# The attention layer of a two-layer decoder trunk: head pairs written out, score tiles in groups of two, and fp32 products on 64x64 blocks

## The reference

```python
kvf = rmsnorm(h, kv_norm) @ kv_w
k_sh = head_rmsnorm(kvf[..., :D].reshape(B, T, N_HEADS, HEAD_DIM), k_norm)
v_sh = kvf[..., D:2 * D].reshape(B, T, N_HEADS, HEAD_DIM)
c_all = jnp.cumsum(jax.nn.log_sigmoid(kvf[..., 2 * D:] + kv_f_bias), axis=1)
...
proj = rmsnorm(h, norm) @ w_in
q = head_rmsnorm(proj[..., :D].reshape(B, S, N_HEADS, HEAD_DIM), q_norm)
z = proj[..., D:]
logits = q @ k.T * scale + cq[..., None] - ck[:, :, None, :]
p = softmax(where(key_pos <= q_pos, logits, -inf))
out = h + ((p @ v) * silu(z)) @ w_out
```

## Time and profile before

| | us |
|---|---|
| median of 3 runs | 2184.94 (2183.36 to 2185.37) |
| the profiled execution's own time | 2185.29 |
| its span, first to last instruction | 2183.6 |
| TensorE busy | 1980.7 |
| VectorE busy | 1026.8 |
| ScalarE busy | 1011.5 |
| GpSimd busy | 239.0 |

### The profile page before, as it was taken

One profiled execution on the slowest core, in us unless ns is written; L12 is line 12 of the kernel. 1 busy time (PEld: TensorE's weight loads), 2 busy tenths in 40 slices (PEclk: granted clock), 3 DMA queues, 4 the chain that ended last, 5 costly groups with the idle time before them and its releaser, 6 DMA issues.

```text
span 2183.6 us, 58287 instructions
## 1 busy us (share of the span) xinstructions
PE 1980.7 (91%) x24895; PEld 1699.7 (78%) x24895; DVE 1026.8 (47%) x1967; ACT 1011.5 (46%) x1735; POOL 239.0 (11%) x253
## 2 busy tenths in 40 slices
PE   5699999999999999999699699999999999998798
PEld 4688988888898988888498477777777777777477
DVE  3656566666666565665523633333333333333421
ACT  3445444444445454444311436464646555565511
POOL 0011111111111111111000201011010101010000
PEclk9899999999999999999689889999999999999799
DMA  5101010000101010100142101010000101000233
GB/s 196 49 2 44 8 36 18 24 27 17 36 8 44 8 46 8 37 15 22 64 139 70 61 21 29 30 29 29 19 29 19 39 10 39 19 29 10 77 116 116
DMA packets 103578, 89.46 MB, mean 41 GB/s; under 512 B 3973, under 2 KB 95736, under 8 KB 103112
## 3 DMA queue, kind: packets, MB, share of 16 engines
q1 hardware_dynamic: 100120, 68.50, 10.7%
q0 software_dynamic: 3040, 17.14, 2.0%
q10 hardware_dynamic: 208, 0.66, 0.1%
HBM read 64.96 MB, written 21.33 MB: 40 GB/s over the span
## 4 chain that ended last, share of the span: by engine, by line
PE 75%; DVE 9%; ACT 8%; issue 5%; DMA 2%; ACTq 0%; SPq 0%; DVEq 0%; POOLq 0%
PE ps L1666 6%; PE ps L1978 6%; PE ps L1979 6%; PE ps L1980 6%; PE ps L2055 5%; PE ps L1668 5%; PE ps L1667 5%; PE ps L1770 4%; PE ps L1602 3%; PE ps L1604 2%; PE ps L1603 2%; PE ps L1799 2%; PE ps L2013 2%; PE ps L2039 2%; PE ps L1794 2%
## 5 line engine op out<-in xcount | busy, mean ns | idle before, releaser
L1666 PE MATMUL ps<-xh,wh 128*128 128x258 f32 (+1 forms) x1024 | 327.8, 320 | 7.5 <-ACT arena L871 3.5
L1667 PE MATMUL ps<-xh,wl 128*128 128x258 f32 (+1 forms) x1024 | 291.0, 284 | 0.0
L1668 PE MATMUL ps<-xl,wh 128*128 128x258 f32 (+1 forms) x1024 | 290.8, 284 | 0.0
L1978 PE MATMUL ps<-xh,wh 128*128 128x348 f32 x768 | 260.1, 339 | 19.8 <-ACT arena_b L1096 14.5
L1979 PE MATMUL ps<-xh,wl 128*128 128x348 f32 x768 | 254.6, 332 | 0.0
L1980 PE MATMUL ps<-xl,wh 128*128 128x348 f32 x768 | 253.9, 331 | 0.0
L1551 DVE TENSOR_REDUCE arena_b<-ps 128x1 f32<-128x144 f32 (+4 forms) x224 | 106.7, 505 | 269.4 <-PE ps L2017 156.8
L1666 PEld LDWEIGHTS ps<-xh,wh 128*128 128x128 f32 x1024 | 193.3, 189 | 26.0 <-ACT arena L871 5.9
L1667 PEld LDWEIGHTS ps<-xh,wl 128*128 128x128 f32 x1024 | 194.1, 190 | 2.6
L2055 PE MATMUL ps<-arena_b 128*128 128x512 f32 (+4 forms) x448 | 186.3, 500 | 9.8 <-ACT arena_b L1120 9.8
L1668 PEld LDWEIGHTS ps<-xl,wh 128*128 128x128 f32 x1024 | 193.5, 189 | 0.0
(11 more groups left out here) (252 smaller groups left out, 4359.7 us busy)
## 6 DMA issues: line engine op xcount, KB each, us to landing
wr<-in_w_in SPq DMA_DIRECT2D x33, 512.0 KB, 4.1
xt_scr<-arena POOLq DMA_DIRECT2D x2, 4176.0 KB, 13.3
wr<-in_kv_w SPq DMA_DIRECT2D x16, 512.0 KB, 4.0
wr<-in_b_w_in SPq DMA_DIRECT2D x16, 512.0 KB, 3.8
arena<-xt_scr SPq DMA_DIRECT2D x8, 522.0 KB, 4.6
arena<-oa_scr SPq DMA_DIRECT2D x8, 520.0 KB, 3.6
arena<-in_x SPq DMA_DIRECT2D x8, 512.0 KB, 3.5
wr<-in_w_out SPq DMA_DIRECT2D x8, 512.0 KB, 3.7
```

The source lines that it names most:

```text
L1666: pe.matmul(bank, wh[:, j, k, :], xh[:, k, t], start=(k == 0), stop=False)
L1667: pe.matmul(bank, wl[:, j, k, :], xh[:, k, t], start=False, stop=False)
L1668: mm = pe.matmul(bank, wh[:, j, k, :], xl[:, k, t], start=False, stop=(k == KO - 1))
L1978: pe.matmul(bank[:, 0:SEG], wh[:, slot, k, :], xh[:, k, t], start=(k == 0), stop=False)
```

## The change

It does the following, in the attention layer alone:

- The loop over pairs is written out on all engines.
- The 14 units of a head go in eight groups (`GROUPS`), mostly of two. The order is: what `fill` holds for the group, the scores of the next group into both score banks, then the weighted sums of this group. The scores of a group wait for all exponentials of the one before. `pt` has four buffers.
- A projection chunk is issued in two halves of 12 products, between which other steps can stand.
- A weighted sum over 128 keys becomes four products of 64 keys by 64 output rows, on the four 64x64 blocks of the array. The two halves of the keys go to two banks, `B_PV[0]` and `B_PV[1]`, and both banks serve every query block. At the end of a block ScalarE copies the first bank to `ob` and `den`, and VectorE adds the second.
- Ln and Exp of the sum of weights are done once per head over 1024 columns, beside those of the sums of squares (`den`, `rsq`). The gate is applied head by head (`gated`), and each head's half is stored by itself.
- A sum of squares is two products on the two diagonal 64x64 blocks.
- `stack` is cut into `stackk` and `stackq`, and all steps get new places.

```diff
-        ARENA_B = 12780
+        ARENA_B = 13848
...
-        pt = [carve_b(512) for _ in range(3)]
-        dln = carve_b(512)
-        ob = carve_b(SEQ)
+        pt = [carve_b(512) for _ in range(4)]
+        ob, den = carve_b(SEQ), carve_b(SEQ)
...
+        GROUPS = [(0, 1), (2, 3), (4,), (5, 6), (7, 8), (9, 10), (11, 12), (13,)]
+        def proj(j, i, *between):
+            return [("proj", j, i, 0), *between, ("proj", j, i, 1)]
         def order(e, more):
...
+            maxima = iter([("smax", 1 - e, i) for i in range(NS)])
+            def m(n):
+                return [next(maxima) for _ in range(n)]
+            fill = [[] for _ in GROUPS]
+            if e == 0:
+                fill[0] = [("vrow", 1, 0), ("vrow", 1, 1), ("stackk", 1), ("stackq", 1)]
+                if more:
+                    fill[1] = proj(0, 0)
+                    fill[2] = m(2) + proj(0, 1, *m(2))
+                    fill[3] = m(2) + proj(0, 2, *m(2))
+                    fill[4] = ([("sumsq", 0, i) for i in range(3)] + [("den", 1), ("rsq", 0)] + m(1) + proj(1, 0, *m(2)))
+                    fill[5] = [("norm", 0)] + m(2) + proj(1, 1, *m(1))
+                    fill[6] = [("maxrow", 1)] + proj(1, 2) + [("gated", 1)]
+                    fill[7] = [("gate",)]
+                else:
+                    fill[1] = [("wsplit",)]
+                    fill[2] = m(3)
+                    fill[3] = m(3) + [("orow", 0)]
+                    fill[4] = m(3) + [("den", 1), ("orow", 1)]
+                    fill[5] = m(3) + [("gated", 1), ("orow", 2)]
+                    fill[6] = m(2) + [("gate",), ("orow", 3)]
+                    fill[7] = [("maxrow", 1)]
+            elif more:
+                fill[0] = [("sumsq", 1, i) for i in range(3)] + [("den", 0), ("rsq", 1)] + proj(2, 0) + [("stackk", 0)]
+                fill[1] = proj(2, 1) + [("norm", 1), ("stackq", 0)]
+                fill[2] = proj(2, 2) + [("gated", 0)]
+                fill[3] = [("vrow", 0, 0), ("vrow", 0, 1)] + m(2) + proj(3, 0, *m(2))
+                fill[4] = m(2) + proj(3, 1, *m(2))
+                fill[5] = m(2) + [("proj", 3, 2, 0)] + m(2)
+                fill[6] = m(2) + [("wsplit",)]
+                fill[7] = [("maxrow", 0), ("proj", 3, 2, 1)]
+            else:
                 for i in range(3):
...
+                    fill[1 + i] = [("orow", 4 + i)]
+                fill[2] = [("den", 0), ("gated", 0)] + fill[2]
+            steps = [("scores", e, 0)]
+            for g in range(len(GROUPS)):
+                steps += fill[g]
+                if g + 1 < len(GROUPS):
+                    steps += [("scores", e, g + 1)]
+                steps += [("weighted", e, g)]
             return steps
...
-            def store_ob(p, dst):
-                pool.wait_ge(S.o_gated, p + 2)
-                pool.dma_start(dst, ob).then_inc(S.ob_stored, 16)
-                pool.wait_ge(S.ob_stored, 16 * p + 16)
+            def store_ob(p, e):
+                pool.wait_ge(S.o_gated, 2 * p + e + 2)
+                pool.dma_start(ob_scr[p][head(e), :], ob[head(e), :]).then_inc(S.ob_stored, 16)
+                pool.wait_ge(S.ob_stored, 16 * (2 * p + e) + 16)
                 pool.sem_inc(S.ob_free, 1)
             for j in range(2, 4):
                 scale_b(0, j)
             scale_b(1, 0)
...
+            for p in range(KO - 1):
+                scale_b(p + 1, 1)
+                scale_b(p + 1, 2)
+                if p:
+                    store_ob(p - 1, 1)
+                scale_b(p + 1, 3)
+                store_ob(p, 0)
+                if p + 2 < KO:
+                    scale_b(p + 2, 0)
...
-                        if i == 2:
-                            act.wait_ge(S.b_evac, n_ + 1)
-                            act.activation(brs, brs, ACT.Exp, scale=-0.5).then_inc(S.hn_rstd, 1)
-                    elif kind == "stack":
+                    elif kind == "den":
+                        n_ = 2 * (p - st_[1]) + st_[1]
+                        if n_ >= 0:
+                            act.wait_ge(S.pv_free, 4 * n_ + 4)
+                            act.activation(den[head(st_[1]), :], den[head(st_[1]), :], ACT.Ln).then_inc(S.d_ln, 1)
+                            if ("rsq", 1 - st_[1]) not in steps:
+                                act.wait_ge(S.d_ln, n_ + 1)
+                                act.activation(den[head(st_[1]), :], den[head(st_[1]), :], ACT.Exp, scale=-1.0)\
+                                    .then_inc(S.d_recip, 1)
+                    elif kind == "rsq":
+                        j = st_[1]
+                        act.wait_ge(S.b_evac, chunk(p, (L_SK, L_SQ)[j]) + 3)
+                        act.activation(brs, brs, ACT.Exp, scale=-0.5).then_inc(S.hn_rstd, 1)
+                        n_ = 2 * p - 1 + j
+                        if ("den", 1 - j) in steps and n_ >= 0:
+                            act.wait_ge(S.d_ln, n_ + 1)
+                            act.activation(den[head(1 - j), :], den[head(1 - j), :], ACT.Exp, scale=-1.0)\
+                                .then_inc(S.d_recip, 1)
+                    elif kind == "stackk":
...
+                        if p + e > 0:
+                            act.wait_ge(S.pv_done, NU * (2 * p + 1 - e))
...
+                        e, g = st_[1:]
+                        for i, w in enumerate(GROUPS[g]):
+                            n_k, q0, n_q, _, _ = unit(w)
+                            n_ = NU * (2 * p + e) + w
+                            act.wait_ge(S.st_done, n_ + 1)
+                            if n_ >= 4:
+                                act.wait_ge(S.pv_done, n_ - 3)
+                            act.activation(pt[n_ % 4][0:n_k, 0:n_q], ps[0:n_k, B_ST[i], 0:n_q], ACT.Exp,
+                                           scale=SCALE).then_inc(S.p_exp, 1)
                     elif kind == "weighted":
-                        e, w = st_[1:]
+                        e, g = st_[1:]
+                        w = GROUPS[g][-1]
                         qb_, kt = UNITS[w]
                         if kt == 4 * qb_ + 4:
                             b, o = slice(e * HD, (e + 1) * HD), slice((1 - e) * HD, (2 - e) * HD)
-                            n_ = 4 * p + 2 * e + qb_
-                            act.wait_ge(S.pv_done, 2 * NU * p + NU * e + w + 1)
-                            act.wait_ge(S.o_norm, n_ + 2)
-                            act.activation(dln[b, :], ps[o, B_PV[qb_], :], ACT.Ln).then_inc(S.d_ln, 1)
-                            act.wait_ge(S.d_ln, n_ + 1)
-                            act.activation(dln[b, :], dln[b, :], ACT.Exp, scale=-1.0).then_inc(S.d_recip, 1)
-
-            def c_rows_of(head):
-                return c_scr[bass.ds(head, 1)].rearrange("a b t -> (a b) t")
+                            c = slice(qb_ * 512, (qb_ + 1) * 512)
+                            if qb_ == 0:
+                                act.wait_ge(S.ob_free, max(2 * p + e, 1))
+                                if p:
+                                    act.wait_ge(S.o_scaled, 2 * p + e - 1)
+                            act.wait_ge(S.pv_done, NU * (2 * p + e) + w + 1)
+                            for dst, rows_ in ((den[b, c], o), (ob[b, c], b)):
+                                act.activation(dst, ps[rows_, B_PV[0], :], ACT.Copy).then_inc(S.pv_read, 1)
...
-                            b = slice(e * HD, (e + 1) * HD)
-                            dve.wait_ge(S.d_recip, 4 * p + 2 * e + qb_ + 1)
-                            if e == 0 and qb_ == 0:
-                                dve.wait_ge(S.ob_free, p + 1)
-                            dve.tensor_tensor(ob[b, qb_ * 512:(qb_ + 1) * 512], ps[b, B_PV[qb_], :], dln[b, :], ALU.mult)\
-                                .then_inc(S.o_norm, 1)
-                            if e and qb_:
-                                dve.wait_ge(S.o_norm, 4 * p + 6)
-                                dve.wait_ge(S.bz_gate, p + 1)
-                                dve.scalar_tensor_tensor(ob, ob, 0.5, zg[:, META:T], ALU.mult, ALU.mult)\
-                                    .then_inc(S.o_gated, 1)
+                            b, o = slice(e * HD, (e + 1) * HD), slice((1 - e) * HD, (2 - e) * HD)
+                            c = slice(qb_ * 512, (qb_ + 1) * 512)
+                            dve.wait_ge(S.pv_done, NU * (2 * p + e) + w + 1)
+                            dve.wait_ge(S.pv_read, 8 * p + 4 * e + 2 * qb_ + 2)
+                            for dst, rows_ in ((den[b, c], o), (ob[b, c], b)):
+                                dve.tensor_tensor(dst, ps[rows_, B_PV[1], :], dst, ALU.add).then_inc(S.pv_free, 1)
+                    elif kind == "gated":
+                        b, q_ = head(st_[1]), p - st_[1]
+                        n_ = 2 * q_ + st_[1]
+                        if n_ >= 0:
+                            dve.wait_ge(S.d_recip, n_ + 1)
+                            dve.wait_ge(S.pv_free, 4 * n_ + 4)
+                            dve.scalar_tensor_tensor(ob[b, :], ob[b, :], 0.5, den[b, :], ALU.mult, ALU.mult)\
```

(68 more changed lines are left out.)

170 lines of the change are left out of this document (61 added, 109 removed).

## The result

The changed kernel takes 2198.39 us (median of 5, 2196.28 to 2202.29) beside 2184.94 us for the kernel before (median of 5): a ratio of 1.0065, 95% interval 1.005 to 1.008. It is 0.65% slower, where 2154 us was forecast and 2189 us was the upper end.

A forecast was written before the change was run, and what follows sets the result against it. TensorE, busy 91% of the span, was taken as the bound, through its work, idle time and low clock. Seven pairs at -2.8 (-20) and the last pair's -11 made -31 on 2185.29 us: 2154 us, range 2119 to 2189.

The forecast's parts named there:

- TensorE's work, +3.0 forecast: Per steady pair, 15 array-shape round trips add 5.4 us and blocks give back 2.4: net 3.0 us more.
- The trip: TensorE's change to 64x64 blocks and back, priced at 0.36 us per round trip, 15 per pair.
- The 2.4 us that blocks should give back: Four 64x64 blocks side by side save 0.07 us per fp32 product, 2.4 us per pair.
- The stalls, -7.9 and +5.0: TensorE's idle time per steady pair: 7.9 us of old waits go, 5.0 us of new ones come.
- the 2.4 us stall: TensorE's per-pair wait on the copy of transposed v, behind Ln/Exp table loads; claimed to go.
- the walk: Stepping through each engine's new order with profiled durations to find new waits: 5.0 us per steady pair, bounds 2 to 8.
- The low clock, -2.9 forecast: 1.2 GHz stretches go once no idle stretch exceeds 2 us: 2.9 us of work time per steady pair regained.
- The last pair, -11 forecast: Last head pair: even head 28 us, odd head 27 us, together 11 us less, from 5 to 16.
- B: Next block's first weighted product waits for copies and adds on the shared banks, 5.8 us more per pair: 2195 us, chance 0.13.
- D: Matmuls in strict program order make four steps per block product, 15.8 us more per pair: 2280 us, chance 0.03.
- C: Idle time only moves: new waits of 8, 1 us low clock kept, last pair -5: 2188 us, chance 0.08.
- the written-out loops: Attention pair loops written out: 0 to 0.3 us per pair less, taken as 0.

The follow-up runs named there:

- trips: Whole-array weighted sums and sums of squares, one extra 16-column product ahead of each projection chunk: whole-array 2196.61 us, as two 64x64 blocks 2201.8 us.
- w_full: Changed kernel with weighted sums as whole-array products, still two banks with copies and adds: 2173.58 us.
- one_bank: w_full with one bank for each query block, emptied by ScalarE's copies alone, no VectorE adds: 2161.6 us.
- combined_wait: combined with TensorE's order for the scores put back, so the third sum of squares of q waits 2 us again: 2160.33 us.
- q_sums_apart: Changed kernel with TensorE taking the odd head's scores of units 2 and 3 ahead of q's third sum of squares: 2183.24 us.
- combined: one_bank plus whole-array sums of squares plus the earlier scores of q_sums_apart: 2141.2 us.
- q_wait_filled: combined_wait with 34 useless products of 112 bf16 columns issued into the 2 us wait ahead of q's third sum: 2149.16 us.
- before_unrolled: Kernel before the change with only its attention pair loops written out on all four engines: 2183.12 us.
- halves_joined: combined with the maxima ahead of a projection instead of between its halves, in all places but one: 2163.08 us.

## Why the prediction was wrong

By its sum for a steady pair, +3.0 - 7.9 - 2.9 + 5.0 = -2.8, against +1.7 measured: 4.5 us a pair, 31 in seven. With the 11 of the last pair that is nearly all of the 44 us between 2154 and 2198.

- **TensorE's work, +3.0 forecast, +3.5 measured: near in sum, wrong in both terms.** The trip was priced at 0.36 us and costs 0.13 to 0.20 (trips; w_full's 2.5 us over the 13 trips that it takes away). The rows had it between products of other types, so half of that price is the fp32 product's own, which the whole-array form pays as well. The 2.4 us that blocks should give back do not exist: 612 ns either way. The table splits the 3.5: the weighted sums in blocks 2.5 (w_full), their second bank with its adds 0.5 (one_bank against w_full; why it costs TensorE work stays open), the sums of squares in blocks 0.5 (combined_wait against one_bank). That leaves 89.8, the 89.9 of before: the new order by itself costs TensorE no work, and neither do the halved projections. The Trainium skill (TensorEngine Tiling (Array Packing), Key Properties) says that a change of the tiling mode drains the engine and gives no price; by the two timelines it is 0.15 us here, and 0.13 to 0.20 over all places.
- **The stalls, -7.9 and +5.0: -2.9 forecast, -1.4 measured.** Not all went that should: "so the 2.4 us stall goes" left 1.0 us at the v copy (line 2027), since the two exponentials and two copies ahead of it take longer than the short products that cover them; and of the 1.6 us at the maxima 0.5 stays even without adds (one_bank). Of the waits that were to come, the walk had 2.4 at the sums of squares (2.5 measured) and 1.4 at the adds (1.4 at the reductions in all, 1.0 of it the adds'), and 0.9 at q's projection, which is absent. It missed 0.7 on the unit of 16 keys (line 2119) and 0.5 at the scores of line 2093.
- **The low clock, -2.9 forecast, -0.3 measured: the step that failed.** "With no idle stretch above 2 us I expect the 1.2 GHz stretches to go as well" was no reading of a row; no row told a stretch of 2.4 us from one of 1.8. The walk itself put 1.8 us of idle time at the sums of squares of q, and it was 1.99. That wait keeps most of the low clock in place: shortened to 1.0 us, low clock falls by 2.2 us a pair (q_sums_apart), put back it costs 2.1 (combined_wait against combined), filled it gives back 1.4 (q_wait_filled). With 2.6 of the 4.5 us a pair this is the largest miss.
- **The last pair, -11 forecast, +0.1 measured.** The walked even head of 28 us took 35.1 (2027.28 to 2062.38), and the odd head's 27 took 30.1; from the first score on that is 65.2 us for 66.7, so 1.6 less, which the products ahead of that score took back (3.2 us for 1.5). The walk let VectorE serve the reductions in time; the adds and splits ahead of them gave waits of 2.4 and 2.7 us, and the clock's records show 10 us at 0.50 from the first of them on (2037.7 to 2048.0). one_bank takes 3.3 us off this pair; moving the splits alone takes nothing.
- **The rivals.** B, slower with 2195 us, had the size and not the place: no wait of a first weighted product on the adds shows in the steady pairs, one of 1.2 us in the last. D is refuted by 612 ns. C came nearest, "idle time only moves" with "one low-clock stretch kept", but it had 1 us of low clock kept where 2.6 of the 2.9 stayed, and the last pair at -5.
- **No change expected, none found:** the written-out loops (before_unrolled). The stores were not tested by themselves; no wait of TensorE or ScalarE on POOL stands in the seven pairs.

Without the blocks and adds and with the q wait halved, the same regrouping is 2.1% faster than before, more than the 1.4% that was looked for. The regrouping was right, fewer table loads among its parts (no run tests them alone); the blocks, the adds and the one wait of 2 us were what it could not afford.

## What to carry to other kernels

Price a stall with the clock that hangs on it: here 1.0 us off a wait of 2 us took 2.1 to 2.2 us of low clock with it. Look for the longest wait that is left in the new order before counting such a gain, and take it for a suspect, not for a rule: halves_joined had low stretches without any wait above 1.0 us. Cutting a product that fills the whole array into blocks gained nothing here: four blocks beside each other took the time of the one product, plus 0.13 to 0.20 us for each trip to the shape and back and, where the halves of the sum land in two banks, an add that stands ahead of other work. A hand walk that had the waits at the sums of squares to 0.1 us still missed three others, and in the last pair what stood ahead in the helper engine's queue: walk that too.

## What was not expected of the hardware

- Useless products in an idle stretch sped the kernel up by 11 us (0.5%), by the granted clock alone.
- The 1.0 us waits of line 2027 are followed by a low stretch in five pairs of seven where a 2 us wait stands 20 us ahead of them, in three where that wait is filled with products (q_wait_filled), in one where it is 1.0 us too (q_sums_apart) and in none of combined. Alone, then, they seldom bring it, but halves_joined has five low stretches behind waits of 0.5 to 1.0 us alone. How waits add up stays open.
- A product of 16 fp32 columns between products of another type costs about 0.2 us whole and 0.4 in blocks, though in the timeline above its second pass starts 0.08 us behind its first, and the next product 0.11 us behind that.
